# A hybrid attention, RWKV-7, HGRN-2 and mixture-of-experts step on one core: mixers in another order, router on undivided rows, buffers regrouped, loads reordered

## What is computed

```
mod   = silu(c) @ w_mod + b_mod            # shift1, scale1, gate1, shift2, scale2, gate2, each (1024) per stream
h     = rms_norm(x, norm_mix_g) * (1 + scale1) + shift1
mix   = concat(attention(h @ w_in), rwkv7(h @ w_in), hgrn2(h @ w_in))      # w_in is 1024 x 3200
x     = x + gate1 * (mix @ w_out)
h     = rms_norm(x, norm_ffn_g) * (1 + scale2) + shift2
logits = h @ router_w + router_b                                           # 32 experts
top_logit, top_idx = top_k(logits, 4);  gates = softmax(top_logit)
moe   = sum over the 4 experts of gate * (clamped_swiglu(h @ w_gu[e] + b_gu[e]) @ w_down[e] + b_down[e])
x     = x + gate2 * moe
y     = rms_norm(x, final_norm_g)
```

## Time and profile before

| what | us |
|---|---|
| median of 3 runs | 1275.15 |
| lowest and highest | 1272.76, 1277.76 |
| profiled execution, its own time | 1273.2 |
| span of the profile, first to last instruction | 1271.4 |
| TensorE busy | 1176.2 (93%) |
| VectorE busy | 314.8 (25%) |
| ScalarE busy | 210.6 (17%) |

### The profile page before, as it was taken

One profiled execution on the slowest core, in us unless ns is written; L12 is line 12 of the kernel. 1 busy time (PEld: TensorE's weight loads), 2 busy tenths in 40 slices (PEclk: granted clock), 3 DMA queues, 4 the chain that ended last, 5 costly groups with the idle time before them and its releaser, 6 DMA issues.

```text
span 1271.4 us, 17024 instructions
## 1 busy us (share of the span) xinstructions
PE 1176.2 (93%) x7124; PEld 474.1 (37%) x7124; DVE 314.8 (25%) x644; ACT 210.6 (17%) x360; POOL 39.4 (3%) x70
## 2 busy tenths in 40 slices
PE   4979998888999999999999999999999999999995
PEld 1425577664433333333333333333333333333321
DVE  1203758644212112111211111111211111111113
ACT  1102254521111111111111111111111111111112
POOL 0200100000000000000000000000000000000000
PEclk9989999898999999999999999999999999999998
DMA  9899000159699999999999999999999999999992
GB/s 372 305 329 390 13 2 14 66 198 418 261 404 431 428 429 428 428 428 429 429 429 429 430 428 430 429 429 429 429 429 429 430 428 429 430 430 430 429 428 124
DMA packets 44397, 460.16 MB, mean 362 GB/s; under 512 B 5129, under 2 KB 7345, under 8 KB 16577
## 3 DMA queue, kind: packets, MB, share of 16 engines
q1 hardware_dynamic: 41296, 451.98, 84.6%
q0 software_dynamic: 2576, 6.41, 1.8%
q10 hardware_dynamic: 480, 1.13, 0.2%
HBM read 458.03 MB, written 1.47 MB: 361 GB/s over the span
## 4 chain that ended last, share of the span: by engine, by line
PE 59%; DMA 33%; DVE 5%; issue 1%; ACT 1%; SPq 0%; ACTq 0%; DVEq 0%
DMA ring<-in_moe_w_gu_dram 27%; PE bank L1222 22%; PE bank L1246 13%; PE bank L604 5%; PE bank L1180 3%; PE bank L1165 3%; DMA ring<-in_w_mod_dram 3%; PE bank L1202 2%; DMA ring<-in_w_in_dram 1%; PE bank L579 1%; DMA proj<-in_norm_ffn_g_dram 1%; PE bank L1173 1%; PE bank L718 1%; DVE proj L2124 1%; PE bank L592 1%
## 5 line engine op out<-in xcount | busy, mean ns | idle before, releaser
L1222 PE MATMUL bank<-ring,proj 128*64 128x512 f32 x1536 | 341.5, 595 | 17.2 <-DMA ring<-in_moe_w_gu_dram 16.1
L1222 PEld LDWEIGHTS bank<-ring,proj 128*64 128x64 f32 x1536 | 105.7, 137 | 250.5 <-issue 209.6
L1246 PE MATMUL bank<-ring,proj 128*64 128x512 f32 x768 | 175.4, 598 | 8.4 <-DVE proj L2124 8.4
L2115 DVE TENSOR_SCALAR proj<-bank 128x512 f32<-128x512 f32 x32 | 22.1, 692 | 462.0 <-PE bank L1222 462.0
L1586 ACT ACTIVATE proj<-proj 128x512 f32<-128x512 f32 x32 | 20.2, 630 | 590.0 <-DVE proj L2115 590.0
L604 PE MATMUL bank<-ring,param_sb 128*128 128x512 f32 (+2 forms) x224 | 89.6, 555 | 0.2 <-DMA ring<-in_w_in_dram 0.2
L1246 PEld LDWEIGHTS bank<-ring,proj 128*64 128x64 f32 x768 | 51.4, 136 | 98.7 <-issue 93.8
L2128 DVE COPY proj<-bank 128x512 f32<-128x512 f32 x32 | 22.1, 691 | 247.9 <-PE bank L1246 247.9
L1180 PE MATMUL bank<-proj 64*128 64x512 f32 x256 | 63.6, 615 | 0.8 <-DVE proj L2128 0.8
L1222 PE MATMUL bank<-param_sb,proj 128*64 128x512 f32 x256 | 57.9, 594 | 6.0 <-DMA param_sb<-in_moe_w_gu_dram 6.0
L1165 PE MATMUL bank<-h_nat,proj 128*64 128x512 f32 x264 | 62.3, 592 | 0.9 <-DVE proj L2097 0.9
(11 more groups left out here) (343 smaller groups left out, 919.3 us busy)
## 6 DMA issues: line engine op xcount, KB each, us to landing
ring<-in_moe_w_gu_dram SPq DMA_DIRECT2D x96, 2048.0 KB, 31.3
ring<-in_moe_w_down_dram SPq DMA_DIRECT2D x48, 2048.0 KB, 35.2
const_sb<-in_moe_w_gu_dram SPq DMA_DIRECT2D x16, 2048.0 KB, 31.3
param_sb<-in_moe_w_gu_dram SPq DMA_DIRECT2D x16, 2048.0 KB, 32.2
ring<-in_w_mod_dram SPq DMA_DIRECT2D x12, 2048.0 KB, 15.4
const_sb<-in_moe_w_down_dram SPq DMA_DIRECT2D x8, 2048.0 KB, 35.2
param_sb<-in_moe_w_down_dram SPq DMA_DIRECT2D x8, 2048.0 KB, 35.2
ring<-in_w_in_dram SPq DMA_DIRECT2D x5, 2048.0 KB, 17.3
```

The lines of the kernel that those rows point to most:

```text
L1222: mm = pe.matmul(b[CAP * half:CAP * half + CAP, :], xT[:, k % 4, k // 4, :], w[:, 2048 * kc + o + 512 * half:2048 * kc + o + 512 * half + ...
L1246: mm = pe.matmul(b_down[CAP * half:CAP * half + CAP, :], aT[:, k % 4, k // 4, :], w[:, D * kc + 512 * half:D * kc + 512 * half + 512], sta ...
L2115: ts(moe["glu"], bank[4][:, :], LIMIT, None, ALU.min).then_inc(sem("glu_sb"), 1)
```

## The change

It has four parts, in the words of the code.

**Order of the mixers.** On VectorE, ScalarE and, at three places, TensorE the calls stand in another order: `rw_gates(1)` behind `project(5)` and `rw_pairs(0)`, `hg_gates(1)` ahead of `rw_level_w(0, 3)`, `at_heads_norm(1)` ahead of `rw_level_w(0, 5)`, `at_heads(1)` ahead of `hg_scores(0, 2)`, `hg_log(1)` right behind stream 0's, `rw_finish(0)` and `hg_finish(0)` behind level 4 of stream 1, `at_sum(1)` earlier. In the front TensorE takes `project(3, 0)` ahead of `modulation("mod", 2)`, and POOL no longer waits for w_in piece 2 before the eleven parameters.

**Router on undivided rows.** norm_ffn_g is multiplied into the scale2 row before the rows are written out (`gain_rows`). After the output projection, u = x * gain is what TensorE turns, in halves; logits are (u @ router_w) * rstd + (shift2 @ router_w + router_b). The second term is made in the front (`shT`, `router_rows`), written to DRAM and read back on all partitions (`router_add`). The sum of squares is taken in halves, and the root is now of 1/variance times D. Top-4 runs stream by stream (`choose`), the gates' softmax behind the one-hot of the first expert, and the barrier is gone. Thirteen padding products become three.

**HGRN's buffers by when they die.** E, qkT, kf, sg and kh fill place 0 of the ring exactly, the others lie in place 1. `hot`, `hotg`, `scat` and `gateT` move to `mod_sb`.

**Loads in order of release.** SyncE issues home 0 when the last `hg_products` is done, half of gate2 before the output projection, home 1 at `hg_done`, w_out's lower half and gate1 in swapped order, home 3 when both upper halves of the output projection of stream 1 are done (the projection now takes the upper rows first).

The diff, cut to what matters:

```diff
-    jobs += [("h2T", s, h) for s in range(2) for h in range(2)]
-    jobs += [("router",), ("pos",)]
+    jobs += [("h2T", 0, 0), ("h2T", 0, 1), ("h2T", 1, 0), ("router", 0), ("h2T", 1, 1), ("router", 1), ("pos",)]
...
-        hg = carve(slots(0, 2), [("kf", 512), ("sg", 512), ("qkT", 768), ("E", 1792), ("U", 2560), ("inter", 512),
-                                 ("attD", 512), ("attO", 256), ("kh", 512), ("st", 256)])
+        hg = carve(slots(0, 2), [("E", 1792), ("qkT", 768), ("kf", 512), ("sg", 512), ("kh", 512),
+                                 ("U", 2560), ("inter", 512), ("attD", 512), ("attO", 256), ("st", 256)])
...
                 sp.wait_ge(sem("mod_sb"), g + 1)
+                if g == 2:
+                    sp.wait_ge(sem("gain_rows"), 1)
...
             ring_load(3, w_out[:, 4:8, :])
+            sp.wait_ge(free[jobs["rw_T", 1, 1, 1] % ROT], jobs["rw_T", 1, 1, 1] // ROT + 1)
+            for s in range(2):
+                spread(gate1[:, s, :], 2 * D, s, "gate1_in")
             sp.wait_ge(sem("at_done"), 1)
             sp.wait_ge(sem("cache_out"), 32)
             ring_load(4, w_out[:, 0:4, :])
-            sp.wait_ge(free[jobs["rw_T", 1, 1, 1] % ROT], jobs["rw_T", 1, 1, 1] // ROT + 1)
-            for s in range(2):
-                spread(gate1[:, s, :], 2 * D, s, "gate1_in")
-            sp.wait_ge(sem("hg_done"), 1)
+            sp.wait_ge(sem("hg_qL"), 8)
             sp.wait_ge(sem("hg_out"), 16)
             expert_load(0, 0, 0)
-            expert_load(0, 1, 1)
+            after(sp, "mixT", 0, 1)
+            spread(gate2[:, 0, :], 5 * D, 0, "gate2_in")
...
+            sp.wait_ge(sem("hg_done"), 1)
+            expert_load(0, 1, 1)
             sp.wait_ge(sem("mixed"), 2)
             for s in range(2):
                 spread(scale2[:, s, :], 4 * D, s, "mod2_in")
-            sp.dma_start(ffn_g, a["norm_ffn_g"][0].unsqueeze(0).to_broadcast([P, D])).then_inc(sem("mod2_in"), 16)
...
+            sp.wait_ge(sem("out_upper"), 1)
+            expert_load(0, 3, 3)
             sp.wait_ge(full[jobs["out", 1, 1] % ROT], jobs["out", 1, 1] // ROT + 1)
-            expert_load(0, 3, 3)
             expert_load(0, 4, 4)
...
-            slot, times = FRONT_AT["in", 2]
-            pool.wait_ge(ring_full[slot], 16 * times)
...
+            def router_rows():
+                after(pe, "shT")
+                b = open_bank(pe, "shW")
+                shT = early["modT"].rearrange("p (c q m) -> p c q m", c=4, q=4)
+                for c in range(KC):
+                    mm = pe.matmul(b[0:2, 0:NE], shT[:, c % 4, 2 + c // 4, 0:2], router_w[:, c, :], start=(c == 0), stop=(c == KC - 1))
+                filled(mm, "shW")
...
+            pool.wait_ge(sem("router_row"), 1)
+            pool.dma_start(bias_dram, router_row).then_inc(sem("router_row_out"), 16)
+            pool.wait_ge(sem("router_row_out"), 16)
+            pool.dma_start(router_add, bias_dram.unsqueeze(0).to_broadcast([P, 2, NE])).then_inc(sem("router_add_in"), 16)
...
             modulation("mod", 1)
             project(2, 1)
+            project(3, 0)
             modulation("mod", 2)
-            project(3, 0)
...
+            dve.wait_ge(sem("ffn_in"), 32)
+            dve.wait_ge(sem("mod_sb"), 3)
+            stt(out=mod_sb[0:64, 2, :], in0=mod_sb[0:64, 2, :], scalar=1.0, in1=mod_sb[0:64, 0, :],
+                op0=ALU.add, op1=ALU.mult).then_inc(sem("gain_rows"), 1)
...
+            turn_u(0, 0)
+            turn_u(0, 1)
+            turn_u(1, 0)
+            router(0)
+            keep_busy(1)
+            turn_u(1, 1)
+            router(1)
+            keep_busy(1)
...
+            def residual(s, part):
+                o, k = slice(512 * part, 512 * part + 512), 2 * s + part + 1
+                b = take(dve, "out", s, part)
+                step(tt(gate1[:, s, o], gate1[:, s, o], b[:, :], ALU.mult))
+                done(dve.nop(), "out", s, part)
+                tt(x[:, s, o], x[:, s, o], gate1[:, s, o], ALU.add).then_inc(sem("x2"), 1)
+                dve.wait_ge(sem("x2"), k)
+                if k == 1:
+                    dve.wait_ge(sem("mod2_in"), 16 * 4)
+                tt(sc[:, s, o], x[:, s, o], sc[:, s, o], ALU.mult).then_inc(sem("u2"), 1)
...
+            residual(0, 0)
+            residual(0, 1)
+            variance(0)
+            residual(1, 0)
+            rows2(0)
+            residual(1, 1)
+            dve.wait_ge(sem("router_add_in"), 16)
+            variance(1)
+            choose(0)
+            rows2(1)
+            choose(1)
```

275 lines of the change are left out of this document (142 added, 133 removed).

## The result

The changed kernel takes **1246.85 us**, the median of 4 runs (1241.51 to 1248.33), against 1274.22 for the kernel before in the same comparison: a ratio of 0.9769, 95% interval 0.9744 to 0.9795, so 27 us or 2.3% faster. A second set of 5 runs of it gave 1245.31 (1242.63 to 1248.45), ratio 0.9757. The forecast was 1247 with a range of 1238 to 1262. The profiled execution took 1247.24 us with a span of 1245.5, against 1271.4.

The account below looks back on a forecast made before the run. The expert weight stream at 429 GB/s was taken to set the end, a constant after TensorE's first release. Terms -14.5 - 7.5 - 6 = -28 took 1275.15 to 1247 us, range 1238 to 1262.

Parts of the forecast that it names:

- Part 1: Output projection and residual to first expert product: router on undivided rows shortens the 61.4 us stretch by 14.5 us.
- The 1.5 us taken off for handshakes: Residual to first expert product: the raw gain of 16 us cut by 1.5 for handshakes the sum lacks.
- halved again at full clock: Router of stream 0 on TensorE: priced at 1.0 us, a half of 3.88, halved again at full clock.
- The scale rows: Ahead of the router: issued at 283 as before, needed on the path about 303, covered with some 10 us to spare.
- Part 2: The front: TensorE's 6.72 us wait for modulation piece 2 and its half clock go, -7.5 us net, bounds 0 and -9.5.
- the loads keep up: Front, after projection 3: ring places come free 5 to 7 us apart, against 4.9 us a piece.
- Part 3: The mixers: stream 1's heads, gates and logarithm done in stream 0's stretch, -6 us net, bounds +1 and -8.
- The two waits at 220.75 and 234.82: Mixers, stream 1: TensorE's waits of 2.40 us for rotary heads and 3.33 us for the logarithm go.
- the 1 us allowed for work given back in stream 0: Mixers, stream 0: of the added root, tables and heads' norm 1 us shows, at most 4.
- Expert loads issued earlier gain nothing by themselves: Expert weight stream: all eight pieces are home anyhow before the first release, so earlier issue gains nothing.
- The end is the moment of that first release plus a constant: Expert stream: bringing the first expert product (338.64) forward brings the end forward by as much.
- Rival D: Experts: with less padding the clock stays at 1.2 GHz and the kernel is slower, 1299 for two experts; chance 0.05.

Follow-up runs that it names:

- e3: The changed kernel with front and mixers put back to the old order; router on undivided rows, buffers and loads stay changed: 1260.55 us, ratio 0.9894.
- e2: The kernel before with the new order of the mixers alone on VectorE, ScalarE and TensorE: 1265.99 us, ratio 0.9932.
- e4: The changed kernel with HGRN's buffers and the expert loads back in the old order: 1241.70 us, run again 1241.28.
- e1: The kernel before with the front's edits alone (POOL's wait dropped, projection 3 of stream 0 ahead of modulation piece 2): 1271.63 us, ratio 0.9978.
- after: The changed kernel itself, unaltered, in two sets of runs: 1246.85 us and 1245.31 us.
- e5: The changed kernel with only its first early expert load and the first gate2 row held back to the mixers' last release: 1243.56 us, ratio 0.9765.
- e6: e5 with a useless extra load of the first expert piece at the changed kernel's early place: 1243.08 us.
- e7: The changed kernel with the four products for the down biases moved behind the first expert's down product: 1246.60 us, ratio 0.9786.
- e9: e5 and e8 together, first load held back and idle-filling products added: 1237.67 us, ratio 0.9706 to the kernel before.
- e10: The changed kernel with fourteen useless products of 128x512 ahead of the first expert's first product: 1254.35 us.
- e8: The changed kernel with two idle-filling products of 128x256 in each of TensorE's two last waits ahead of the first expert: 1243.30 us, ratio 0.9763.

## Why the prediction was right, and where not

**Part 1** (forecast -14.5, raw sum -16) measured -16.0, and -16.0 alone in e3. The steps hold: the gather was put 40.1 us behind the output projection and comes 39.8 behind it. The 1.5 us taken off for handshakes were not needed. The router's half was priced at 1.0 us, "halved again at full clock": wrong, each half took 1.94 us, 0.12 a record as before (3.88 for 32); the records before had not been slowed. That the sum still fits is because other steps were a little dear. The scale rows: VectorE waits for them, but under cover, as said:

```profile
278.47 0.69 DVE L2113 TENSOR_TENSOR proj<-x_res,proj 128x512 f32<-128x512 f32 x1 [2.21 <-DMA proj<-mod_rows]
```

**Part 2** (forecast -7.5) measured -5.7 at projection 5 and between -2.7 and -7.7 in the other traces with it. The step that failed is "the loads keep up". Modulation piece 6 is waited for in nine of the eleven traces that have the new front, by 0.64 to 3.30 us, while the DMA engines are full (share 0.98 to 1.04 from 85 to 120 us in the changed kernel). Projection 5 starts anywhere from 117.58 to 122.53 in them, which may be a good part of the spread of the new kernels' runs. The added router product cost 0.63, below the 1.4 taken.

**Part 3** (forecast -6) measured -7.7: -10.1 alone in e2, and -11.8 in e4. The two waits at 220.75 and 234.82 are gone; one of 1.79 us is left in that stretch. The three values agree once the last stretch is taken apart. Before the change it begins with this product:

```profile
262.74 0.51 PE L780 MATMUL bank<-param_sb,ring 64*64 64x64 f32 x10 [0.88 <-ACT param_sb L1356]
```

From projection 5 to it the kernel before takes 137.5 us (e1 and e3, with the mixers in the old order too, 139.0 and 140.1) and all with the new mixers 129.5: -8.0 each time, the far bound of the forecast. From it to the output projection it was 14.5 us, of which 2.18 a gap of TensorE like the one above, with a clock of 0.66 behind it; there e4 gains 3.8, e2 2.1, and the changed kernel loses 0.3. That stretch the prediction did not price. Within the 8.0, the 1 us allowed for work given back in stream 0 did not show. On the tables the row decided rightly for the smaller price. The root moved into stream 0 is loaded and used like this, and the exponentials' table is loaded back behind it:

```profile
182.58 1.28 ACT L1323 ACT_TABLE_LOAD   x1
184.35 0.21 ACT L1323 ACTIVATE small<-small 128x10 f32<-128x10 f32 x1 [0.49 <-DVE small L1679]
184.63 1.28 ACT L1436 ACT_TABLE_LOAD   x1
185.92 0.60 ACT L1436 ACTIVATE ring<-bank 128x512 f32<-128x512 f32 x1
```

The root waits 0.49 us for its operand. The second load starts 0.07 us behind the root, and the exponential 0.01 us behind the load. The Trainium skill, ScalarE: Activation LUTs, "What ACT_TABLE_LOAD costs", adds a drain of 1.38 us to each switch; these rows have no room for one.

**"Expert loads issued earlier gain nothing by themselves"** was right as to the gain, and missed a loss: with the first one, issued at 248.15, TensorE's last stretch of the mixers is 1.2 to 4 us longer. I had asked of that edit only what it brings.

**"The end is the moment of that first release plus a constant"** is the step that was nearly right. First release to end was 929.1 before and is 931.2 after, because the releases behind it came 2.8 us late at the lower clock. What counts is all idle time of the DMA engines before the stream runs unbroken, not the first gap alone. The stream itself was as said, 429 GB/s before and after:

```profile
1003.28 34.17 DMA ring<-in_moe_w_gu_dram
...
1062.06 34.29 DMA ring<-in_moe_w_gu_dram
```

58.8 us for two experts, as in the earlier trace rows.

**Rival D** came in small. The clock did fall from 305 on, where it stands at 1.00 in the first expert of the kernel before, and took 1.4 + 2.8 = 4.1 us of TensorE's time in the first expert (28.6 instead of 24.5 us from first product to thirteenth piece); it did not stay low, as the forecast held. The Trainium skill, TensorE: Matmul & The Clock Gate, "Why this matters for your kernels", warns of idle gaps between bursts, but of longer ones than the 0.70 and 0.67 us that stand here ahead of the first expert, so it does not settle the case. Nor do the traces: eight have these two waits, the clock fell ahead of the ninth piece in five (after twice, e3, e4 twice) and held in three (e5, e6, e7). The prediction also tells the 3.8 us wait at 306.9 and the slow padding at 326.36 as one fall of the clock. They are two: the windows of the kernel before show 0.50 from 310 to 315, 1.00 from 320 to 325 and 0.66 from 325 to 330.

The sum came out right, 28 against 27.4 in the median, because errors cancelled: at the first expert product the changed kernel is 29.4 us ahead (parts 1 and 3 brought 3 us more than forecast, the front 2 less), and the clock took 4.1 of that, so that the thirteenth piece is 25.3 us earlier. The ninth piece went out 5.1 us behind the first expert product and not 3.7, and the span is 1245.5 and not near 1243. That the median then fell within 1 us of the forecast is luck: the four runs are spread over 7 us, and the spans differ by 25.9 us where the medians differ by 27.4.

## What to carry to other kernels

Where a weight stream sets the end, count bytes: the time at the end is what the transfers are behind once they run without a break, so every stretch before that in which the DMA engines stand idle or move little counts; moving work behind one release to bring that release forward gained nothing in e7, since the next releases came later. A load issued early into a home that is free is not free itself: here it brought nothing and went with a longer stretch of small products on TensorE. And price each part together with what stands behind it: three parts alone gave 21 of the 26 us, since each paid for the same slow expert.

## What the runs showed of the hardware

- TensorE stops for 1.0 to 2.2 us, with no semaphore to wait for ("issue"), in stretches of 64x64 products while the DMA engines are busy: 2.12 us in the changed kernel, 1.85, 1.58, 1.30 and 1.03 in others with an expert load beside them, but also 2.18 in the kernel before (at 267.44), 2.13 in e1 and 1.52 in e2, where w_out's lower half and the two gate1 rows were all that had gone out. With that half alone (e4 twice, e5, e9) no gap is over 0.31, though the engines' share is 0.88 to 0.97 in the five us in which most of it lands. How much traffic it takes stays open, and so does the reason. The page of the changed kernel lists a DMA queue for instructions (34 packets, 0.56 MB); that TensorE's instructions come late beside the loads would fit, but no run shows it.
- Behind the gap the granted clock can fall: 0.66 to 0.71 in the last 5 us ahead of the output projection in the changed kernel (twice), e7 and e10, 1.00 in e3, e6 and e8.
- What the slower clock costs in the first expert repeats to 0.01 us in two executions of the changed kernel (23.53 us both times from ninth to thirteenth piece), and yet the clock is 1.00 throughout in e5, e9 and e10. What decides it stays open.
- A 32-bit product leaves two records, so one of 128x512 costs 0.87 us, not the 0.44 of a record: the mistake in the expectation of e10.
